# A two-block transformer on one core: the second block's attention takes its values as stationary operand in two parts, and norms the exponents on GpSimd ahead of the turn

## The chip, the cores and the metric

The kernel runs on one NeuronCore of one Trainium2 chip. The metric is the device time of one execution in microseconds. TensorE (PE) does matmuls and transposes, ScalarE (ACT) activations and copies, VectorE (DVE) elementwise work and reductions, GpSimd (POOL) small loads before this change, and SyncE (SP) issues the weight loads. Each engine runs its own list of instructions strictly in order and waits on semaphores for the others.

## What is computed

512 tokens of width 1024 go through a first block (2 layers) and a second block (2 layers). The change is in the second block's attention alone. Cut to that, for each of its layers:

```python
# fox: 8 heads of 64, causal, with a forget term
s = q @ k.T * scale + c_q[:, None] - c_k[None, :]
o_a = softmax(where(kpos <= qpos, s, -inf)) @ v
# nsa: 8 heads of 64, 2 kv heads; three branches, each with its own gate
o_c = (softmax(where(valid, q @ kc.T, NEG)) * valid) @ vc      # 31 compressed blocks
o_s = softmax(causal(q @ ks.T)) @ vs                           # "selected": all blocks at 512 tokens
o_w = softmax(causal(q @ kw.T)) @ vw                           # window of 512
o_n = g[..., 0:1] * o_c + g[..., 1:2] * o_s + g[..., 2:3] * o_w
mixed = sigmoid(gate_a) * (o_a @ w_o_fox) + sigmoid(gate_b) * (o_n @ w_o_nsa)
x = x + mixed @ w_out
```

## The kernel before

Dense layers run with each float32 operand split into an upper and a lower fp32r part, three matmuls for one (`three`, L568 to L570). Weights come in units of 512 KB; ScalarE makes the upper part `Wh` (L1273) and VectorE the lower part `Wl` (L1883), two units ahead of their use. A unit is 24 matmuls of 512 columns on TensorE.

The order of every engine is written out by hand with generators. The main thread of the program issues the dense layers, and after each 6 of its matmuls calls `tick()`, which lets every open side do one step. The attention is such a side: between two ticks stand 6 dense matmuls (3 short ones in `hidden`), which fill the time in which the attention's own steps wait for other engines. All engines run the same scheme, so that step i of a side stands at the same place of the main thread on each of them. `drain(side)` calls `tick()` with no dense matmuls between until that side is finished.

`attend` handles one item (t, g, h), a block of 128 queries and a head, with t+1 blocks of keys. In step i TensorE turns the exponents of item i-3 (`turn`, L713), makes the scores of item i (`head`, L781 to L784, mask L777) and mixes item i-5 (`mix`, L728). ScalarE makes the exponents of item i with their sum (L1394) and copies the turned exponents of even items out of PSUM (L1408); VectorE takes the maximum of item i (L2072) and copies those of odd items (L2085). In `mix` the turned exponents are stationary (128x128) and 64 columns of values move, all in float32. The sums are inverted once for all heads of a query block, and the output is scaled after the mixing (L2109, L2120), turned back (`turn_out`, L745; `on_side`, L792) and split for the next dense layer.

Per layer of the second block there are 32 fox items and 64 nsa items. The nsa side begins while the first gate layer runs and ends under the last gate layer; the three branches are added on VectorE in SBUF (L2123, L2712), and the compressed branch is a side of its own that runs at the same time (`compressed_side`, values at L1158):

```python
        for s in range(2):
            while (tag, 2 * c + s, 0) not in done:
                yield
            b = fresh(f"co{l} {2 * c + s}")
```

The main thread then waits for the outputs in front of the output projection:

```python
        drain(ont)
        for t in range(0, KD, 2):
            lin_t(f"ob{l} {t}", 4, M.ONh, M.ONl, at_each(f"on{l}") if t == 0 else None)
```

Of the kernel before, what the change touches and what calls it, by code (L numbers as in the profile page):

```python
# [8 lines left out]
F32 = mybir.dt.float32  # L9
# [158 lines left out]
class Memory:  # L168

    def __init__(self, nc, ctx):
# [18 lines left out]
        self.OS = fixed("OS", [2, 512])  # L190
        self.CST = fixed("CST", [C_END])
# [52 lines left out]
        self.QA = [area("QA", [4, S], w, F32R) for w in (6144, 0)]  # L244
        self.KAh = [area("KAh", [4, S], w, F32R) for w in (8192, 2048)]
        self.KAl = [area("KAl", [4, S], w, F32R) for w in (10240, 4096)]
        self.VF = area("VF", [NT, 512], 12288)
        self.OAh = area("OAh", [4, S], 14336, F32R)
        self.OAl = area("OAl", [4, S], 16384, F32R)
        self.FGT = area("FGT", [S], 14336)  # L250
# [4 lines left out]
        self.AK = area("AK", [2, 2, S], 8192)  # L255
        self.QNS = area("QNS", [NT, 512], 10240)
        self.KVS = area("KVS", [NT, 512], 12288)
# [3 lines left out]
        self.QN = area("QN", [8, S], 4096, F32R)  # L261
        self.KSh = area("KSh", [2, 2, S], 8192, F32R)
        self.KSl = area("KSl", [2, 2, S], 10240, F32R)
        self.ONS = area("ONS", [NT, 512], 18432)
# [19 lines left out]
        self.CT = area("CT", [512], 22688)  # L284
# [38 lines left out]
class Signals:  # L323

    def __init__(self, nc, ctx):
# [68 lines left out]
        self.ons = sem("nsa_branches_added")  # L395
# [105 lines left out]

def tiles(x):

    return x if isinstance(x, list) else [x[:, k, :] for k in range(x.shape[1])]
# [39 lines left out]
def tensor_program(pe, M, G, K, plan):  # L544
# [6 lines left out]
    used, pv = Count(G.w_used), Count(G.pv)  # L551
# [215 lines left out]

    def main_part(side, n):
# [10 lines left out]
    def causal(t, b, q, kh, kl, extra=None):  # L779
# [223 lines left out]
    for l in range(DEPTH):  # L1003
# [15 lines left out]
        def fox_scores(t, g, h, b):  # L1019
            return causal(t, b, M.QA[g][:, h, :], M.KAh[g][:, h, :], M.KAl[g][:, h, :], (M.SEL[0:96, 4 * g + h, :], M.CR[0:96, :]))  # L1020
# [10 lines left out]
        def fox_side(*args, **kw):  # L1031
            yield from idle(FOX_WAIT)
            yield from attend(*args, **kw)

        def heads_side(j):
# [7 lines left out]
            else:  # L1043
                pe.wait_ge(G.rk, 2 * l + j - 3)
                turn_rows(f"nk{l} {j - 4}", lambda s: M.KVS[:, s, 256 * (j - 4):256 * (j - 4) + P])
# [5 lines left out]
        def nsa_scores(t, g, h, b):  # L1051
            return causal(t, b, M.QN[:, h, :], M.KSh[:, g, h // 4, :], M.KSl[:, g, h // 4, :])

        def nsa_side():
# [15 lines left out]
            yield from attend(tag, softmax_items(8, (0, 1)), 8, nsa_scores,  # L1070
# [1837 lines left out]
```

## Time and profile before

| | us |
|---|---|
| runs, median of 3 | 2899.51 (2898.21 to 2901.87) |
| the profiled execution | 2900.79 |
| its span, first to last instruction | 2899.0 |
| TensorE busy in the span | 2797.7 |
| VectorE, ScalarE, GpSimd busy | 1435.8, 1161.7, 14.6 |
| granted TensorE clock, mean | 0.984 |

The span is what the trace shows; the 1.8 us around it are the launch. Busy times overlap: matmuls are pipelined, so the start of one to the start of the next is its price in a full stream, and the "mean ns" of one is longer than that. The second block's first layer lies at 1237 to 2080 us, its second one at 2080 to 2899 us, and the two read alike.

### The profile page before, as it was taken

To read this page: it belongs to the slowest core of one execution; us is meant where nothing else is said; L and a number is where in the kernel's file an instruction comes from. 1 tells how busy PE (TensorE), PEld (TensorE's weight loads), DVE (VectorE), ACT (ScalarE), POOL (GpSimd) and SP (SyncE) were. 2 spreads that over 40 slices of the span, in tenths; PEclk is the share of its full clock that TensorE was granted. 3 is DMA by queue.
4 is the path that set the end of the run, shared out by engine and by line. 5 is a ranking of instruction groups with operands and counts; after the bars stand their busy time and mean duration, and the time that the engine had idled before them with its cause. 6 is when DMAs were issued, how large, how long until landed. Compare 5 with 4: busy or idle time off the path is not lost.

```text
span 2899.0 us, 35141 instructions
## 1 busy us (share of the span) xinstructions
PE 2797.7 (97%) x14041; PEld 2316.3 (80%) x14041; DVE 1435.8 (50%) x2435; ACT 1161.7 (40%) x2009; POOL 14.6 (1%) x29
## 2 busy tenths in 40 slices
PE   7999999998999999989999999999999999999997
PEld 6777888887778888778788888888778788888886
DVE  6755433357553433465645553343556545553343
ACT  4554222235542222354656343242354655342231
POOL 1000000000000000000000000000000000000000
PEclk9899999999999999999999999999999999999999
DMA  4102333321023333321311223333312211333332
GB/s 131 43 23 87 95 95 101 95 82 51 23 80 95 101 95 95 91 62 53 97 51 45 87 88 95 101 95 95 84 52 81 73 37 59 98 94 100 95 97 71
DMA packets 186357, 231.43 MB, mean 80 GB/s; under 512 B 11874, under 2 KB 140356, under 8 KB 186196
## 3 DMA queue, kind: packets, MB, share of 16 engines
q1 hardware_dynamic: 184500, 225.95, 25.8%
q0 software_dynamic: 976, 1.32, 0.3%
q8 instruction: 112, 1.84, 0.3%
q10 hardware_dynamic: 720, 1.92, 0.2%
q14 instruction: 49, 0.40, 0.0%
HBM read 227.05 MB, written 2.11 MB: 79 GB/s over the span
## 4 chain that ended last, share of the span: by engine, by line
PE 84%; DVE 9%; ACT 4%; issue 3%; DMA 0%; DVEq 0%; ACTq 0%; SPq 0%
PE bank L568 24%; PE bank L570 24%; PE bank L569 23%; PE bank L728 4%; PE bank L713 2%; DVE Wl L1883 1%; ACT Wh L1273 1%; PE bank L781 1%; PE bank L782 1%; PE bank L665 1%; DVE KAl L1931 1%; PE bank L963 1%; DVE STT L2072 1%; ACT TMP L1394 0%; PE bank L777 0%
## 5 line engine op out<-in xcount | busy, mean ns | idle before, releaser
L1883 DVE TENSOR_TENSOR Wl<-RAW,Wh 128x1024 fp32r<-128x1024 f32 (+3 forms) x434 | 511.3, 1200 | 436.3 <-ACT Wh L1273 435.6
L1273 ACT ACTIVATE Wh<-RAW 128x1024 fp32r<-128x1024 f32 (+3 forms) x434 | 438.3, 1032 | 367.6 <-PE bank L570 367.4
L568 PE MATMUL bank<-Hh,Wh 128*128 128x512 f32 (+1 forms) x976 | 397.6, 407 | 6.6 <-DVE Wl L1883 5.0
L570 PE MATMUL bank<-Hh,Wl 128*128 128x512 f32 (+1 forms) x976 | 383.1, 392 | 0.0
L569 PE MATMUL bank<-Hl,Wh 128*128 128x512 f32 (+1 forms) x976 | 381.9, 391 | 0.0
L568 PE MATMUL bank<-Wh,A 128*128 128x512 f32 x864 | 337.2, 390 | 0.0
L570 PE MATMUL bank<-Wh,A 128*128 128x512 f32 x864 | 336.3, 389 | 0.0
L569 PE MATMUL bank<-Wl,A 128*128 128x512 f32 x864 | 336.2, 389 | 0.0
L568 PE MATMUL bank<-HA,Wh 128*128 128x512 f32 x704 | 276.1, 392 | 7.5 <-DVE HA L1932 7.5
L570 PE MATMUL bank<-HA,Wl 128*128 128x512 f32 x704 | 274.9, 390 | 0.0
L569 PE MATMUL bank<-HA,Wh 128*128 128x512 f32 x704 | 274.9, 390 | 0.0
L568 PEld LDWEIGHTS bank<-Hh,Wh 128*128 128x128 f32 (+1 forms) x976 | 183.4, 188 | 44.5 <-DVE Wl L1883 5.8
L1394 ACT ACTIVATE TMP<-bank,STT 128x512 f32<-128x512 f32 (+1 forms) x240 | 126.6, 529 | 229.0 <-DVE STT L2072 228.2
L570 PEld LDWEIGHTS bank<-Hh,Wl 128*128 128x128 f32 (+1 forms) x976 | 182.7, 187 | 41.6
L568 PE MATMUL bank<-Wh,Hh 128*128 128x512 f32 (+2 forms) x512 | 207.7, 406 | 4.1 <-DVE Wl L1883 2.7
L569 PEld LDWEIGHTS bank<-Hl,Wh 128*128 128x128 f32 (+1 forms) x976 | 183.5, 188 | 34.5
L570 PE MATMUL bank<-Wh,Hl 128*128 128x512 f32 (+2 forms) x512 | 195.0, 381 | 0.0
L569 PE MATMUL bank<-Wl,Hh 128*128 128x512 f32 (+2 forms) x512 | 194.0, 379 | 0.0
L570 PEld LDWEIGHTS bank<-Wh,A 128*128 128x128 f32 x864 | 162.2, 188 | 33.8
L569 PEld LDWEIGHTS bank<-Wl,A 128*128 128x128 f32 x864 | 162.2, 188 | 33.4
L568 PEld LDWEIGHTS bank<-Wh,A 128*128 128x128 f32 x864 | 162.2, 188 | 33.1
L568 PEld LDWEIGHTS bank<-HA,Wh 128*128 128x128 f32 x704 | 132.7, 188 | 36.6 <-DVE HA L1932 8.6
(357 smaller groups left out, 4133.4 us busy)
## 6 DMA issues: line engine op xcount, KB each, us to landing
RAW<-in_w_up_dram SPq DMA_DIRECT2D x108, 512.0 KB, 3.7
RAW<-in_w_down_dram SPq DMA_DIRECT2D x108, 512.0 KB, 3.7
RAW<-in_w_in_dram SPq DMA_DIRECT2D x90, 512.0 KB, 3.6
RAW<-in_w_gate_dram SPq DMA_DIRECT2D x44, 512.0 KB, 3.8
RAW<-in_w_out_dram SPq DMA_DIRECT2D x28, 512.0 KB, 3.7
RAW<-in_cmp_w_dram SPq DMA_DIRECT2D x16, 512.0 KB, 3.8
RAW<-in_w_o_fox_dram SPq DMA_DIRECT2D x8, 512.0 KB, 3.7
RAW<-in_w_o_nsa_dram SPq DMA_DIRECT2D x8, 512.0 KB, 3.4
```

The costliest lines, as they stand in the source:

```text
L568: pe.matmul(o, sh, mh, start=first, stop=False)
L569: pe.matmul(o, sh, ml, start=False, stop=False)
L570: return pe.matmul(o, sl, mh, start=False, stop=last)
L665: i = pe.transpose(b[:, s * P:(s + 1) * P], M.X[:, s, k * P:(k + 1) * P], ident)
L713: x = pe.transpose(b[:, k * P:(k + 1) * P], M.PB[:, i % 4, k * P:(k + 1) * P], ident)
L728: x = pe.matmul(b[:, h * 64:(h + 1) * 64], M.PT[:, i % 3, k * P:(k + 1) * P], values(g, h, kb[k]), start=k == 0, stop=k == len(kb) - 1)
L781: pe.matmul(b[:, 0:w], q[:, t * P:w], kh[:, 0:w], start=True, stop=False)
L782: pe.matmul(b[:, 0:w], q[:, t * P:w], kl[:, 0:w], start=False, stop=extra is None)
L963: pe.matmul(b[:, 0:w], M.MQ[0:96, h, t * P:w], M.MK[0:96, h, 0:w], start=True, stop=True)
L1273: sc.activation(M.Wh[:, v % NHL, 0:n], M.RAW[:, v % NRAW, 0:n], ACT.Copy).then_inc(G.w_hi, 1)
L1394: sc.activation(pb, b[:, 0:w], ACT.Exp, bias=nm, accum_out=sm).then_inc(*K.empties(name))
L1883: ve.tensor_tensor(M.Wl[:, v % NRAW, 0:n], M.RAW[:, v % NRAW, 0:n], M.Wh[:, v % NHL, 0:n].bitcast(F32), ALU.subtract).then_inc(G.w_lo, 1)
```

## The change

Work is arranged in bundles of two items: for fox two query blocks of a head, for nsa two heads of a query block. The exponents `P1` of an item are multiplied with one over their sum (and with the gate, for nsa) by GpSimd before they are turned. The turned ones are split in two fp32r parts, the upper by ScalarE and the lower by VectorE, for every item. In `mix` the values are stationary (128 columns: upper and lower part side by side) and the turned exponents of both items move (up to 256 columns); a second matmul with the upper values alone takes the lower part of the exponents. The output comes out already turned, with its two halves in PSUM rows 0 to 63 and 64 to 127, which ScalarE and VectorE add (`OAy`, `ONS`). The compressed branch is added in the same PSUM bank (`compressed_values`, four matmuls of 128 columns for one query block and kv head), at the last bundle of a bank. The nsa side on every engine waits before such a bundle until the compressed side is done.

The diff, cut to its core:

```diff
@@ PE @@
+    def mixing(B, scores, values, first_mix=None, group=None, extra=None, need=None):
+        def turn(i):
+            b = fresh(f"{tag} t{i}")
+            pe.wait_ge(*norm.due())
+            e = B.exps(M, i)
+            for k in range(len(B.blocks(i))):
+                x = pe.transpose(b[:, k * P:(k + 1) * P], e[:, k * P:(k + 1) * P], ident)
...
+        def mix(n):
...
+            if B.closes(n) and extra:
+                extra(*items[last], b)
...
+            for k in range(len(kb)):
+                ph, c = B.beside(M.PTh, n, k)
+                pl, _ = B.beside(M.PTl, n, k)
...
+                pe.matmul(b[:, c:c + w], v, ph, start=B.opens(n) and k == 0, stop=False, skip_group_check=True)
+                x = pe.matmul(b[0:64, c:c + w], v[:, 0:64], pl, start=False, stop=k == len(kb) - 1, skip_group_check=True)
...
+        for i in range(n + 7):
...
+            c = B.ended(i - 5)
+            if need and c is not None and B.closes(c):
+                while need not in done:
+                    yield
+            if 0 <= i - 3 < n:
+                turn(i - 3)
+            if i < n:
+                head(i)
+            if c is not None:
+                mix(c)
+            yield
-        pe.matmul(b[:, 0:w], q[:, t * P:w], kl[:, 0:w], start=False, stop=extra is None)
+        pe.matmul(b[:, 0:w], q[r:r + 64, t * P:w], kl[r:r + 64, 0:w], start=False, stop=extra is None)
-                for s in range(2):
-                    while (tag, 2 * c + s, 0) not in done:
-                        yield
-                    b = fresh(f"co{l} {2 * c + s}")
...
+            done.add(("compressed", l))
@@ on_side @@
-            for j in range(4):
-                turn_rows(f"on{l} {j}", lambda s: M.ONS[:, s, j * P:(j + 1) * P])
@@ ACT @@
+            upper(B.turned(M.PTh, i), M.bank[K.of(name)][:, 0:len(B.blocks(i)) * P].rearrange("p (k c) -> p k c", c=P), name)
+        def fox_take(t, g, h):
+            sc.activation(M.OAy[64 * (h % 2):64 * (h % 2) + 64, 2 * g + h // 2, :], M.bank[K.of(o)][0:64, :], ACT.Copy).then_inc(G.whole, 1)
@@ DVE @@
+        def invert(n):
+            i = B.ends[n] - 1
+            (t0, _, h0), (t1, _, h1) = B.bundles[n]
+            sums, fac = (M.STT[:, x, t0:t1 + 1, h0:h1 + 1] for x in (1, 4))
+            ve.wait_ge(*K.drained(f"{tag} s{i}"))
+            ve.reciprocal(fac, sums).then_inc(*rec.up())
+        def turn(i):
+            lower(B.turned(M.PTl, i), M.bank[K.of(name)][:, 0:len(B.blocks(i)) * P].rearrange("p (k c) -> p k c", c=P),
+                  B.turned(M.PTh, i)).then_inc(*K.empties(name))
...
+            if 0 <= i - 3 < n:
+                turn(i - 3)
+            c = B.ended(i - 1)
+            if c is not None:
+                invert(c)
+            if i < n:
+                head(i)
@@ fox_k, lower part of the keys @@
-                    for r in (0, 64):
-                        i = lower(M.KAl[c][r:r + 64, 2 * j + x, :], M.TQ[64 * x:64 * x + 64, j, :], M.KAh[c][r:r + 64, 2 * j + x, :])
+                    r = slice(64 * x, 64 * x + 64)
+                    i = lower(M.KAl[c][r, j, :], M.TQ[r, j, :], M.KAh[c][r, 2 * j + x, :])
@@ POOL @@
+    def normalise(B, gate):
+        for i, (t, g, h) in enumerate(B.items):
+            if B.place[i][1] == 0:
+                gp.wait_ge(*rec.due())
+            e = B.exps(M, i)
+            fac = M.STT[:, 4, t, h:h + 1]
+            if gate(t, g, h) is None:
+                gp.tensor_scalar(e, e, fac, None, ALU.mult).then_inc(G.norm, 1)
+            else:
+                gp.tensor_scalar(e, e, fac, gate(t, g, h), ALU.mult, ALU.mult).then_inc(G.norm, 1)
```

In the changed kernel's lists the dense matmuls are L643 to L645, the turn is L858, scores L921 and L922, mask L916, mixing L879 (upper) and L880 (lower), compressed values L1299. `P_9` is the exponents, `PT_58` and `PT_59` the two parts of the turned ones.

First, TensorE at the end of the nsa side. Before, near the end of the side of the first layer:

```order
L713 MATMUL bank<-CST_57,TMP_55 128x128 x3
L728 MATMUL bank<-KVS_117,TMP_55 128x64 x3
L568 MATMUL bank<-Hh_50,Wh_54 128x512
L569 MATMUL bank<-Hl_51,Wh_54 128x512
L570 MATMUL bank<-Hh_50,Wl_53 128x512
L568 MATMUL bank<-Hh_50,Wh_54 128x512
L569 MATMUL bank<-Hl_51,Wh_54 128x512
L570 MATMUL bank<-Hh_50,Wl_53 128x512
L713 MATMUL bank<-CST_57,TMP_55 128x128 x2
```

Now, at the same end:

```order
L858 MATMUL bank<-CST_61,P_9_57 128x128 x3
L921 MATMUL bank<-KSh_130,QN_129 128x384
L922 MATMUL bank<-KSl_131,QN_129 128x384
L916 MATMUL bank<-CMB_65,IDB_64 128x128
L879 MATMUL bank<-PT_58,VN_122 128x256
L880 MATMUL bank<-PT_59,VN_122 64x256
L879 MATMUL bank<-PT_58,VN_122 128x256
L880 MATMUL bank<-PT_59,VN_122 64x256
L858 MATMUL bank<-CST_61,P_9_57 128x128 x2
L921 MATMUL bank<-KSh_130,QN_129 128x384
L922 MATMUL bank<-KSl_131,QN_129 128x384
L916 MATMUL bank<-CMB_65,IDB_64 128x128
```

Before, every step had its 6 dense matmuls. Now the side stops after 18 heads (it waits for the compressed side), 30 steps come later with dense matmuls, and the last 17 heads and 20 turns of each layer stand in `drain(ont)` with none between them.

Second, ScalarE and VectorE at the start of a unit of weights in the nsa side (second step after a pair's last exponents). ScalarE before:

```order
L1394 ACTIVATE TMP_55,STT_65<-bank,STT_65 128x128
L1273 ACTIVATE Wh_54<-RAW_52 128x1024
L1394 ACTIVATE TMP_55,STT_65<-bank,STT_65 128x384
L1408 ACTIVATE TMP_55<-bank 128x512
L1394 ACTIVATE TMP_55,STT_65<-bank,STT_65 128x256
```

ScalarE now:

```order
L1582 ACTIVATE P_9_57,STT_69<-bank,STT_69 128x128
L1448 ACTIVATE PT_58<-bank 128x4x128
L1582 ACTIVATE P_9_57,STT_69<-bank,STT_69 128x128
L1402 ACTIVATE Wh_54<-RAW_52 128x1024
L1448 ACTIVATE PT_58<-bank 128x4x128
L1582 ACTIVATE P_9_57,STT_69<-bank,STT_69 128x512
```

VectorE now, at the same place:

```order
L2137 TENSOR_TENSOR PT_59<-bank,PT_58 128x4x128
L2368 TENSOR_REDUCE STT_69<-bank 128x1
L2089 TENSOR_TENSOR Wl_53<-RAW_52,Wh_54 128x1024
L2137 TENSOR_TENSOR PT_59<-bank,PT_58 128x4x128
L2376 RECIPROCAL STT_69<-STT_69 128x2
L2368 TENSOR_REDUCE STT_69<-bank 128x1
```

Both splits of a unit now stand between the last exponents of a pair and the reciprocal of its sums, and a copy of turned exponents is on each engine in every step.

## Rows read from the trace of the kernel before

**Rows 1.** The page: span, and busy time of the engines.

```profile
span 2899.0 us, 35141 instructions
PE 2797.7 (97%) x14041; PEld 2316.3 (80%) x14041; DVE 1435.8 (50%) x2435; ACT 1161.7 (40%) x2009; POOL 14.6 (1%) x29
```

**Rows 2.** Busy time by stretch: stretch and length, busy of each engine, PEclk.

```profile
core 0: us, PE busy (x) PEld busy (x) DVE busy (x) ACT busy (x) POOL busy (x), PEclk, DMA share, GB/s
1237.00:1290.00 53.00, 44.60 (x223) 34.93 (x222) 40.02 (x62) 30.93 (x52) 0.00 (x0) 1.00 0.21 61
1290.00:1390.00 100.00, 99.39 (x588) 82.35 (x587) 53.83 (x103) 43.54 (x93) 0.00 (x0) 1.00 0.21 63
...
1430.00:1500.00 70.00, 66.87 (x436) 56.55 (x436) 32.53 (x70) 45.41 (x95) 0.00 (x0) 0.98 0.19 53
1500.00:1570.00 70.00, 69.80 (x432) 58.94 (x433) 38.95 (x78) 36.08 (x72) 0.00 (x0) 0.97 0.14 39
```

**Rows 3.** The chain of waits in 1237 to 1286 us, shares by line.

```profile
by line: DVE KAl L1931 22.3%; DVE Wl L1883 11.8%; issue 7.2%; ACT KAh L1688 5.1%; ACT Wh L1273 4.1%; DVE TQ L2020 4.1%; DVE STT L2072 3.3%; ACT TMP L1394 2.9%; DVE TMP L2521 2.8%; DVE QA L1931 2.8%; DVE TQ L2022 2.7%; ACT QA L1680 2.6%; ACT
```

**Rows 4.** Groups of instructions on PE by shape, both layers (a float32 matmul leaves two records).

```profile
L728 PE MATMUL bank<-KVS,TMP 128*128 128x64 f32 x640 | 92.5, 275 | 0.1
...
L728 PE MATMUL bank<-VF,TMP 128*128 128x64 f32 x320 | 45.5, 273 | 0.0
...
L1158 PE MATMUL bank<-VCB,CT 128*128 128x256 f32 x32 | 8.8, 396 | 0.4 <-DVE CT L2697 0.4
...
L792 PE MATMUL bank<-CST,ONS 128*128 128x128 f32 x32 | 4.9, 275 | 1.9 <-DVE ONS L2123 1.9
```

**Rows 5.** The chain of waits over the whole run: start, us, what.

```profile
1280.86 0.89 PE bank L728 x8
...
1525.76 0.92 PE bank L1158 x4
```

**Rows 6.** Timeline of PE, short dense matmuls: start, us, what.

```profile
1463.43 0.28 PE L569 MATMUL bank<-Wl,XHL 128*64 128x256 f32 x1
1463.55 0.28 PE L570 MATMUL bank<-Wh,XHL 128*64 128x256 f32 x1
1463.67 0.38 PE L713 MATMUL bank<-CST,TMP 128*128 128x128 f32 x2
```

**Rows 7.** Timeline of one nsa step at the start of a unit.

```profile
1518.28 0.60 PE L713 MATMUL bank<-CST,TMP 128*128 128x128 f32 x4
...
1518.92 0.60 ACT L1408 ACTIVATE TMP<-bank 128x512 f32<-128x512 f32 x1 [0.60 <-PE bank L713]
...
1519.17 0.29 DVE L2072 TENSOR_REDUCE STT<-bank 128x1 f32<-128x128 f32 x1 [0.57 <-PE bank L777]
1519.49 0.37 ACT L1394 ACTIVATE TMP<-bank,STT 128x128 f32<-128x128 f32 x1
...
1519.85 1.05 ACT L1273 ACTIVATE Wh<-RAW 128x1024 fp32r<-128x1024 f32 x1
...
1520.93 1.23 DVE L1883 TENSOR_TENSOR Wl<-RAW,Wh 128x1024 fp32r<-128x1024 f32 x1 [1.47 <-ACT Wh L1273]
...
1521.69 0.27 PE L713 MATMUL bank<-CST,TMP 128*128 128x128 f32 x1
```

**Rows 8.** Groups on ACT, 1237 to 1570 us.

```profile
L1394 ACT ACTIVATE TMP<-bank,STT 128x512 f32<-128x512 f32 x24 | 16.5, 689 | 44.0 <-DVE STT L2072 44.0
...
L1394 ACT ACTIVATE TMP<-bank,STT 128x384 f32<-128x384 f32 x20 | 11.6, 582 | 33.2 <-DVE STT L2072 33.2
L1805 ACT ACT_TABLE_LOAD x9 | 11.5, 1283 | 0.2
```

**Rows 9.** Groups on DVE, 1237 to 1570 us.

```profile
L1931 DVE TENSOR_TENSOR KAl<-TQ,KAh 64x512 fp32r<-64x512 f32 x16 | 11.0, 687 | 3.0 <-ACT KAh L1688 2.8
L2072 DVE TENSOR_REDUCE STT<-bank 128x1 f32<-128x384 f32 x20 | 11.1, 553 | 1.2 <-PE bank L777 0.9
...
L2098 DVE RECIPROCAL STT<-STT 128x4 f32<-128x4 f32 x8 | 1.4, 171 | 0.1
```

**Rows 10.** Timeline of PE about a fall of the clock.

```profile
1496.73 0.28 PE L1132 MATMUL bank<-KCh,QN 128*128 128x32 f32 x1 [0.23 <-ACT TMP L1394]
...
1502.08 0.63 PE L570 MATMUL bank<-OAh,Wl 128*128 128x512 f32 x1
```

**Rows 11.** Groups on POOL over the whole run.

```profile
L2897 POOL MEMSET const-bfloat16-1.0<- 128x1 bf16 x1 | 0.1, 96 | 0.0
```

More of the change, by code:

```diff
@@ L1 @@
 import collections
+import itertools
 from contextlib import ExitStack
@@ L499, in softmax_items, with __init__, blocks, opens @@
     return [(t, g, h) for g in groups for pair in PAIRS for h in range(heads) for t in pair]
+class Bundles:
+    def __init__(self, tag, bundles, out, col):
+        self.tag, self.bundles, self.col = tag, bundles, col
+        self.items = [item for b in bundles for item in b]
+        self.place = [(n, x) for n, b in enumerate(bundles) for x in range(len(b))]
+        self.ends = list(itertools.accumulate(len(b) for b in bundles))
+        self.outs = [f"{tag} o{out(*b[0])}" for b in bundles]
+    def blocks(self, i):
+        return key_blocks(self.tag[:3], self.items[i][0])
+    def opens(self, n):
+        return self.outs[n] not in self.outs[:n]
+    def closes(self, n):
+        return self.outs[n] not in self.outs[n + 1:]
+    def ended(self, i):
+        return self.ends.index(i + 1) if i + 1 in self.ends else None
+    def span(self, i):
+        n, x = self.place[i]
+        first = i - x
+        at = n % 2 * (1536 - 512 * len(self.bundles[n]) // 2 if len(self.bundles[n]) == 2 else 768)
+        lo = at + sum(len(self.blocks(j)) * P for j in range(first, i))
+        return lo, lo + len(self.blocks(i)) * P
+    def exps(self, M, i):
+        lo, hi = self.span(i)
+        return M.P1[:, lo:hi]
+    def freed_by(self, i):
+        n, lo, hi = self.place[i][0], *self.span(i)
+        return max((j for j in range(i) if self.place[j][0] == n - 2 and self.span(j)[0] < hi and lo < self.span(j)[1]), default=None)
+    def turned(self, part, i):
+        n, x = self.place[i]
+        m = len(self.bundles[n])
+        at = self.span(i - x)[0]
+        nb = len(self.blocks(i - x + m - 1))
+        return part[:, at:at + nb * m * P].rearrange("p (k x c) -> p k x c", x=m, c=P)[:, 0:len(self.blocks(i)), x, :]
+    def beside(self, part, n, k):
+        b, i = self.bundles[n], self.ends[n] - len(self.bundles[n])
+        x = [len(self.blocks(i + y)) > k for y in range(len(b))].index(True)
+        at = self.span(i)[0] + k * len(b) * P
+        return part[:, at + x * P:at + len(b) * P], self.col(*b[x])
@@ L502, in tiles, with fox_bundles, nsa_bundles @@
+def fox_bundles(l):
+    pairs = [[(t, g, h) for t in pair] for g in range(2) for h in range(4) for pair in ((2, 3), (0, 1))]
+    return Bundles(f"fox{l}", pairs, lambda t, g, h: f"{g}{h}", lambda t, g, h: t * P)
+def nsa_bundles(l):
+    pairs = [[(t, g, h), (t, g, h + 1)] for pair in PAIRS for kv in range(2) for g in range(2) for h in (4 * kv, 4 * kv + 2) for t in pair]
+    return Bundles(f"nsa{l}", pairs, lambda t, g, h: f"{t}{h // 4}", lambda t, g, h: h % 4 * P)
 def tiles(x):
@@ L1731, in nsa_side @@
             yield from idle(5)
-            yield from attend(tag, softmax_items(8, (0, 1)), 8, None)
+            yield from mixing(nsa_bundles(l), take=nsa_take, need=("compressed", l))
         def hidden(kv):
@@ L2620, in nsa_side @@
             yield from idle(5)
-            yield from attend(tag, softmax_items(8, (0, 1)), 8, None)
+            yield from mixing(nsa_bundles(l), add_up=nsa_sum, need=("compressed", l))
         def hidden(kv):
```

334 lines of the change are left out of this document (235 added, 99 removed).

## Prediction, made before the changed kernel ran

> **What bounds the kernel now.** I read the page first: TensorE is busy in 2797.7 of 2899.0 us [rows 1], so time taken from its stream is time gained, unless something else moves in. Next the busy time by stretch. In the fox stage (1290 to 1390 us) TensorE is busy 99.39 of 100 us, and where nsa runs under dense layers 69.80 of 70 us, while ScalarE and VectorE are about half busy [rows 2]. The reader should see that half-busy engines cause no wait today because each has two to three steps of slack: exponents of item i are turned at step i+3, copies are used at step i+5. At the front of fox (1237 to 1290 us) it is otherwise: 8.4 us idle on TensorE [rows 2], and the chain of waits runs through VectorE, with `KAl` the largest piece [rows 3]. So three questions decide: what leaves TensorE's stream, whether the new chain of waits still fits the slack, and whether dense matmuls still stand between the steps.
>
> **TensorE's own work, per layer.** Old mixing leaves 640 and 320 records over both layers [rows 4], 480 a layer, at 0.89/8 = 0.111 us [rows 5]: 53 us. New mixing, counted from the diff: 160 matmuls for nsa and 64 for fox with 256 columns, 32 for fox with 128. The trace has no such matmul of a value tile, but the short dense ones with 256 moving fp32r columns start 0.12 us apart [rows 6]. A bound from below is half of it for the 64-column stationaries (128 matmuls, 8 us less), from above 0.15. I take 0.12: 31 us, 22 saved. The turns of the outputs (16 for nsa, 16 for fox) go: 32 records of `ONS` in both layers [rows 4], about 0.09 each, so 3 us. The compressed values cost 16 records of 0.92/4 = 0.23, 4 us at most [rows 4, 5]; now 32 float32 matmuls of 128 columns, 64 records at the 0.11 of L728, 7 us: 4 lost. Sum: 21 us less a layer, **42 us less**. The shorter contraction of `kl` I cost at nothing: the same columns move.
>
> **The front of fox.** 8 of 16 `KAl` instructions of 0.69 us go [rows 9], on the engine that is the chain there; the split of the fox values adds about 1.4 us to it earlier. I take 3.5 us a layer, **7 us less**; bounds 0 and 5.5.
>
> **The new chain.** The step in front of the turn is now: last exponents of a pair (ScalarE), copy of the turned item before it (ScalarE), its lower part and then the reciprocal (VectorE, in this order in its list), norm (GpSimd), turn (TensorE). From the start of an odd step I add rows [rows 7, 9]: 0.64 until the copy of four turned blocks starts, copy 0.60, lower part 0.69 (a VectorE instruction of 512 columns), maximum 0.29, exponents 0.37, and, where a unit begins there, `Wh` 1.05 and `Wl` 1.23, then the next lower part 0.69, reciprocal 0.17, norm. GpSimd's multiplication is in no row. Below it lies its memset, 0.1 us [rows 11]; above it `Wl`, which is twice as long in elements and two-input, 1.23 us. I take what VectorE needs for the same shapes, 0.3 us at 128 columns and 0.55 to 0.7 above [rows 7, 9], being the nearest. With some 0.3 us of hand-overs this is 6.3 us, 3.8 without the splits. The two TensorE steps that must cover it hold 12 dense matmuls of 0.23 and 1.9 us of attention, 4.7 us. So an ordinary pair is hidden, and each unit of weights that begins between the last exponents and the reciprocal costs 1.5 us. Queued behind the waiting turn are the scores, and behind these everything of the next step.
>
> The Trainium skill (GPSIMD Engine Reference, section 3.1) gives 769 ns for one input of 512 elements; by it the norm of the longest items would be 0.1 us longer than mine and the sum about 3 us higher, an estimate. No row here shows it.
>
> Fox: the pieces are wider (exponents of four blocks 0.69 [rows 8], scores with four matmuls) and a 64-row copy of the output stands ahead of `Wh`: 6.9 us against 5.2 of cover. 7 units fall so: **12 us a layer**. In the first 18 steps of nsa two stretches of four steps have only 3 short dense matmuls (0.36 us), so a pair has 2.7 us of cover against 3.8 to 4; with four unit starts I take **9 us a layer** net of what waits there now (3.1 us idle, [rows 2]). The 30 later filled steps have the units at the harmless place in the pair, but both sigmoids of each gate layer, with table loads of 1.28 us on either side [rows 8], stand ahead of a copy or the next exponents: some 3 us in 8 steps, **10 us a layer**. Together 31 a layer, **62 more**.
>
> **The end of nsa without cover.** The side stops after 18 heads until the compressed side is done, about 30 ticks. These dense matmuls are then missing at the end: 17 heads and 20 turns a layer stand in `drain(ont)` alone. A pair is now its chain: turn and scores 0.7, reading 0.2, maximum 0.5, exponents 0.53 (between 384 and 256 columns, [rows 8, 9]), copy 0.45, lower part 0.5, reciprocal 0.17, norm 0.45, hand-overs 0.3: 3.8 to 4 us, ten pairs, 39 us. TensorE's work in it is 23 us (50 turned blocks at 0.107, 17 scores at 0.45, 54 mixings at 0.12, compressed values 3.6). So 16 us idle, plus 2.4 at the end, where the last copy, the sum and two splits stand in front of the output projection, which before were hidden by the last gate layer (none of it idle today, [rows 2]): 18.4 a layer, **37 more**.
>
> **The clock.** Today a stretch of small matmuls after short idle times is followed by one at the lower level: at 1502.08 us a 512-column matmul takes 0.63 us [rows 10] where 0.40 is usual, and the clock means 0.98 and 0.97 there [rows 2]. The uncovered end is 40% idle, so I expect it to fall there, partly under the chain's own waits, and one fall of today to be gone: net 2 a layer, **4 more**.
>
> **The sum.** 2899.0 - 42 - 7 + 62 + 37 + 4 = 2953 us of span; with the 1.8 us around it 2955. The profiled execution (2900.79) is 1.3 us above the median of the runs (2899.51). Hence **2954 us**, 1.9% slower.
>
> **Rivals.**
> *Only the savings* (faster, 6%): the waits stay hidden, the end too. 2899.5 - 49 = 2851 us. For it: engines half busy. Against: latency, not busy time, is what the new chain lacks; ScalarE was already waited for when it only had exponents.
> *Only the uncovered end costs* (10%): in the filled steps the split of a unit finds room, because ScalarE runs ahead of TensorE. Then -49 + 37 + 4: 2892 us. It decides on the 1.5 us: if `Wh` could begin before the odd step's exponents, there is no stall. The list has it behind them.
> *Longer norms and a low clock* (20%): GpSimd at the upper bound, 0.5 more in each of some 35 binding pairs a layer (+32), and the whole end at 1.2 GHz, turn and scores doubled in ten pairs and some us after it (+18): 3004 us. A mechanism for the first part is VectorE holding what GpSimd reads through: 38 `Wl` of 1.23 us lie among 333 us, and a norm behind one waits up to that long. The Trainium skill (SBUF — State Buffer, section "SBUF: two separate sides") states such an exclusive lock between a VectorE instruction with two SBUF inputs and a GpSimd instruction; no run here has shown it, for GpSimd computes nothing today.
> *The gain and the loss cancel* (4%).
> The forecast has the remaining 60%; its own range is 2920 to 2985 (chain stalls between half and one and a half times mine).
>
> **Numbers.** The range takes in the forecast, the case with the uncovered end alone, and most of the one with longer norms: 2890 to 3010. What repeats of this kernel can tell from no change is about 0.2%, 6 us. Slower: 0.60 + 0.20 + a little = 0.81; within 0.2% 0.05; faster 0.14, from the first two rivals.
>
> **What would show it.** Right: L879 and L880 start 0.12 us apart; idle of TensorE ahead of L858, ended by GpSimd, of 1 to 2 us at unit starts in fox; an end of nsa of about 40 us a layer with TensorE some 60% busy, ahead of the output projection; GpSimd busy 80 to 150 us; no idle at the compressed side. Wrong: if L858 never waits in fox, the chain is shorter than I added; if mixing takes 0.2 us a matmul, the saving is gone and the time lies above 2985; if the end of nsa is under 30 us a layer, the pair's chain overlaps more than I think.

## The result, and the profile after

The changed kernel takes **3053.99 us** (median, 3052.99 to 3055.3), the kernel before 2898.95 us beside it: ratio 1.0533, 95% interval 1.0515 to 1.0551. It is 5.3% slower where 1.9% was forecast, and lies outside the range of 2890 to 3010 us. The direction was right, the size was not.

The page of the profile after, the lines that answer to [rows 1]:

```profile
span 3051.2 us, 34802 instructions
PE 2855.3 (94%) x13625; PEld 2309.7 (76%) x13625; DVE 1476.4 (48%) x2551; ACT 1225.5 (40%) x2166; POOL 163.2 (5%) x221
```

There are 416 fewer TensorE records than before, and yet TensorE is busy 58 us longer. So two things went wrong at once: its own work did not shrink, and it idles besides. To see both, I cut the first layer into the stretch from the first fox score to the last and the stretch from the first nsa score to the output projection. After (the third row is the end of nsa that has no dense matmuls to cover it, without its first wait: the last dense matmul ends at 1639.6 us), then before, as busy time by stretch:

```profile
core 0: us, PE busy (x) PEld busy (x) DVE busy (x) ACT busy (x) POOL busy (x), PEclk, DMA share, GB/s
1262.60:1379.70 117.10, 94.10 (x463) 68.70 (x463) 57.54 (x111) 56.35 (x127) 32.75 (x30) 0.93 0.13 37
1439.50:1696.40 256.90, 224.09 (x1102) 168.97 (x1102) 115.74 (x252) 135.42 (x282) 38.45 (x64) 0.89 0.15 44
1643.50:1696.40 52.90, 44.05 (x187) 30.83 (x186) 21.58 (x56) 23.13 (x68) 10.92 (x19) 0.65 0.00 0
```

```profile
1263.70:1355.00 91.30, 85.72 (x522) 69.28 (x523) 49.04 (x93) 47.87 (x109) 0.00 (x0) 1.00 0.16 47
1415.90:1620.30 204.40, 199.03 (x1229) 167.21 (x1230) 103.32 (x207) 115.53 (x228) 0.00 (x0) 0.98 0.18 51
```

Fox is 26 us longer and nsa 52.5. Idle (length less busy) grew from 5.6 to 23.0 us in fox and from 5.4 to 32.8 us in nsa: 45 of the 78. The granted clock fell from 1.00 and 0.98 to 0.93 and 0.89, and to 0.65, mostly the 1.2 GHz level, in the uncovered end. The rest is busy time, longer in part by that clock. By start-to-start times of the records, idle taken off, in these stretches (mixing in fox before includes 0.8 us of turned outputs):

| us, first layer | before | after |
|---|---|---|
| scores with `kh` and `kl`, fox / nsa | 11.8 / 25.3 | 21.6 / 50.5 |
| mixing, fox / nsa | 14.7 / 34.9 | 9.7 / 29.2 |
| compressed values | 3.0 | 9.0 |
| turns of exponents, fox / nsa | 6.2 / 13.9 | 7.4 / 17.5 |
| dense, fox / nsa | 46.2 / 104.6 | 49.7 / 104.3 |

The scores stand out: 35 us more a layer, in a part that the prediction costed at nothing. TensorE's longest waits after:

```profile
engine line waited for: us in total, times, longest us
PE bank L858 <- POOL P L3128: 54.9, 47, 4.1
PE bank L858 <- POOL P L3126: 30.0, 16, 9.5
PE bank L921 <- DVE OAy L2833: 7.4, 6, 1.3
PE bank L1285 <- DVE CB L2970: 7.4, 4, 2.6
```

L858 is the turn and waits for GpSimd's norm, 85 us in both layers; the prediction had the place and 62 us of such stalls. The fourth row is the turn of the compressed branch's exponents, which waited for nothing before. What a norm takes, by shape (x and mean ns of one):

```profile
L3126 POOL TENSOR_SCALAR P<-P,STT 128x512 f32<-128x512 f32 x16 | 27.8, 1740 | 0.0
L3128 POOL TENSOR_SCALAR P<-P,STT,GS 128x512 f32<-128x512 f32 x32 | 24.4, 771 | 289.4 <-DVE STT L2376 289.4
...
L3128 POOL TENSOR_SCALAR P<-P,STT,GS 128x128 f32<-128x128 f32 x32 | 14.1, 450 | 96.9 <-DVE STT L2376 96.9
L3126 POOL TENSOR_SCALAR P<-P,STT 128x128 f32<-128x128 f32 x16 | 9.6, 603 | 60.6 <-DVE STT L2376 60.6
```

The nsa form, with two scalars, takes 771 ns at 512 columns. The Trainium skill gives 769 ns, measured, for 512 elements of one input at best (GPSIMD Engine Reference, section 3.1), and the trace agrees. The fox form, with one scalar, takes 1740 in the mean, which neither that page nor my range had.

One stall of fox, start to end, in the timeline after (start, us, engine):

```profile
1317.30 0.69 ACT L1582 ACTIVATE P<-bank,STT 128x512 f32<-128x512 f32 x1 [1.43 <-DVE STT L2368]
...
1317.81 0.38 PE L858 MATMUL bank<-CST,P 128*128 128x128 f32 x2
...
1318.10 0.59 ACT L1883 ACTIVATE OAy<-bank 64x512 f32<-64x512 f32 x1
...
1318.54 0.36 PE L879 MATMUL bank<-PT,VF 128*128 128x256 f32 x1
1318.72 1.06 ACT L1402 ACTIVATE Wh<-RAW 128x1024 fp32r<-128x1024 f32 x1
...
1318.74 0.28 PE L880 MATMUL bank<-PT,VF 128*64 128x256 f32 x1
1318.86 0.28 PE L879 MATMUL bank<-PT,VF 128*128 128x256 f32 x1
...
1319.68 0.37 ACT L1448 ACTIVATE PT<-bank 128x256 fp32r<-128x256 f32 x1
...
1319.81 1.23 DVE L2089 TENSOR_TENSOR Wl<-RAW,Wh 128x1024 fp32r<-128x1024 f32 x1 [0.39 <-ACT Wh L1402]
...
1321.07 0.42 DVE L2137 TENSOR_TENSOR PT<-bank,PT 128x256 fp32r<-128x256 f32 x1
1321.41 0.16 DVE L2376 RECIPROCAL STT<-STT 128x2 f32<-128x2 f32 x1
...
1321.66 3.26 POOL L3126 TENSOR_SCALAR P<-P,STT 128x384 f32<-128x384 f32 x2 [5.90 <-DVE STT L2376]
...
1323.05 0.52 PE L858 MATMUL bank<-CST,P 128*128 128x128 f32 x3 [2.00 <-POOL P L3126]
```

The reader should see that the exponents are ready at 1318.0 and the norm begins at 1321.66: the output's copy, `Wh`, the turned copy, `Wl` and the lower part stand ahead of a reciprocal of 0.16 us. That is the chain that the prediction named. (The mixing in between starts 0.20 us apart once and then 0.12.)

### The profile page after: what moved, and what is told of

Same layout as the page of the kernel before. It is cut to its first block and busy times, and to the rows that moved or that the text cites. A ratio compares the mean times of both kernels' runs of the same rounds, so it can differ in the third digit from the quotient of the medians.

```text
span 3051.2 us, 34802 instructions
## 1 busy us (share of the span) xinstructions
PE 2855.3 (94%) x13625; PEld 2309.7 (76%) x13625; DVE 1476.4 (48%) x2551; ACT 1225.5 (40%) x2166; POOL 163.2 (5%) x221
## 5 line engine op out<-in xcount | busy, mean ns | idle before, releaser
L643 PE MATMUL bank<-Hh,Wh 128*128 128x512 f32 (+1 forms) x976 | 394.3, 404 | 5.9 <-DVE Wl L2089 4.3
L645 PE MATMUL bank<-Hh,Wl 128*128 128x512 f32 (+1 forms) x976 | 385.3, 395 | 0.0
L643 PE MATMUL bank<-Wh,A 128*128 128x512 f32 x864 | 337.2, 390 | 0.0
L645 PE MATMUL bank<-Wh,A 128*128 128x512 f32 x864 | 336.3, 389 | 0.0
L643 PE MATMUL bank<-HA,Wh 128*128 128x512 f32 x704 | 276.7, 393 | 7.2 <-DVE HA L2138 7.2
L645 PE MATMUL bank<-HA,Wl 128*128 128x512 f32 x704 | 275.5, 391 | 0.0
L643 PEld LDWEIGHTS bank<-Hh,Wh 128*128 128x128 f32 (+1 forms) x976 | 184.9, 189 | 45.4 <-DVE Wl L2089 5.1
L645 PEld LDWEIGHTS bank<-Hh,Wl 128*128 128x128 f32 (+1 forms) x976 | 184.3, 189 | 41.6
L643 PE MATMUL bank<-Wh,Hh 128*128 128x512 f32 (+2 forms) x512 | 206.7, 404 | 4.1 <-DVE Wl L2089 2.7
L2137 DVE TENSOR_TENSOR PT<-bank,PT 128x384 fp32r<-128x384 f32 (+1 forms) x192 | 94.3, 491 | 229.6 <-ACT PT L1448 228.7
L645 PE MATMUL bank<-Wh,Hl 128*128 128x512 f32 (+2 forms) x512 | 195.0, 381 | 0.0
L645 PEld LDWEIGHTS bank<-Wh,A 128*128 128x128 f32 x864 | 162.2, 188 | 33.8
L643 PEld LDWEIGHTS bank<-Wh,A 128*128 128x128 f32 x864 | 162.2, 188 | 33.2
L858 PE MATMUL bank<-CST,P 128*128 128x128 f32 x480 | 99.2, 311 | 89.8 <-POOL P L3128 54.9
```

What stands on the lines that cost most here:

```text
L643: pe.matmul(o, sh, mh, start=first, stop=False)
L645: return pe.matmul(o, sl, mh, start=False, stop=last)
L858: x = pe.transpose(b[:, k * P:(k + 1) * P], e[:, k * P:(k + 1) * P], ident)
L2137: return ve.tensor_tensor(lo, src, h.bitcast(F32), ALU.subtract)
```

## The experiments

All ratios are to the kernel before, run beside them, with their 95% intervals. e7, e8, e9, e15 and e17 leave out parts of the result and only measure; the others compute all of it. "Beyond the bound" means that the intervals of two kernels don't overlap.

### The contraction of `kl`

```
e1: the changed kernel
-        pe.matmul(b[:, 0:w], q[r:r + 64, t * P:w], kl[r:r + 64, 0:w], ...)
+        pe.matmul(b[:, 0:w], q[:, t * P:w], kl[:, 0:w], ...)
e2, e2b: the kernel before
-        pe.matmul(b[:, 0:w], q[:, t * P:w], kl[:, 0:w], ...)
+        pe.matmul(b[:, 0:w], q[0:64, t * P:w], kl[0:64, 0:w], ...)     # e2
+        pe.matmul(b[:, 0:w], q[0:96, t * P:w], kl[0:96, 0:w], ...)     # e2b
```

> The changed kernel with one edit: the matmul with the lower parts of the keys contracts over all 128 rows again (it then adds the query's lower part times the lower part of the other head's keys, a term of the size of rounding). Theory A (the 64-row matmul costs, because every item pays some 0.28 us more from score to score, 96 items a layer): the 512-column kl matmul goes back from 0.43 to about 0.24 us start to start and the kernel loses about 50 us, to 3000 to 3010 us. Rival B (the 64-row matmul only fills time in which TensorE would have waited for GpSimd): waits for GpSimd grow by as much, and the time stays at 3040 to 3055 us.

> The kernel before with one edit: its kl matmul contracts over rows 0 to 63 alone, as in the change; what it leaves out is the product of the two lower parts. Theory A: in this kernel, where TensorE is the bound, it costs 0.28 us an item, 192 items, so about 54 us: 2950 us. Rival (the extra time belongs to the change of row halves between heads or to another row of the new order): no more than 5 us, 2900 to 2905 us.

> The kernel before with its kl matmul over rows 0 to 95, as the forget-gate matmul of fox already does with its 96 rows. If any contraction below 128 rows costs, this gives the same as the 64-row one, about 2950 us. If only one of at most 64 rows does, since the 96-row forget-gate matmul next to it never showed more than its columns, 2900 us.

Measured: e1 3031.63 us (1.0464, 1.0443 to 1.0486), 22 us less; e2 2938.51 (1.0138, 1.0122 to 1.0154), 39 us more in a kernel that has nothing else of the change; e2b 2900.1 (1.0004, 0.9994 to 1.0013), no change. One item in the timeline of e2, then the same item in e2b:

```profile
1290.13 0.42 PE L781 MATMUL bank<-KAh,QA 128*128 128x384 f32 x1
1290.48 0.44 PE L782 MATMUL bank<-KAl,QA 64*128 64x384 f32 x1
1290.86 0.34 PE L784 MATMUL bank<-CR,SEL 96*128 96x384 bf16 x1
```

```profile
1289.28 0.42 PE L781 MATMUL bank<-KAh,QA 128*128 128x384 f32 x1
1289.54 0.34 PE L782 MATMUL bank<-KAl,QA 96*128 96x384 f32 x1
1289.72 0.34 PE L784 MATMUL bank<-CR,SEL 96*128 96x384 bf16 x1
```

From L781 to L782 0.35 us instead of 0.26, from L782 to L784 0.38 instead of 0.18: 0.29 us for this item. By the medians of e2 against before it is 0.28 to 0.29 us at 256 to 512 columns and 0.23 at 128, so it hardly grows with the columns. The Trainium skill has a rule for it (TensorEngine Tiling (Array Packing), section "Tiling Modes", key properties: changing the tiling mode drains the TensorE; 64 rows are a mode, 96 are not one). For rows the runs agree; the same section lists stationaries of 64 columns as a mode too, and there they show no such price (L879 and L880 alternate at 0.12 us above). Over e2 the scores grew by 52 us, 0.27 an item, and 9 us less idle time took part of it back: 39. In e1 the busy time of both stretches fell by 30 us a layer, but their length by only 8.5, since idle took its place: the turns now waited 121 us for GpSimd instead of 85. So theory A had the mechanism, and B's waits took more than half of it back: the time lies between the ranges of the two. In the kernel before, 39 us came where A said 54.

### The norm and what stands around it

From here all start from e1 with a second scalar in the norm of fox (e4), but for e3, which has the second scalar alone; where GpSimd's norm is left out, there is no second scalar to add.

```
e3, e4 (GpSimd):
-                gp.tensor_scalar(e, e, fac, None, ALU.mult)
+                gp.tensor_scalar(e, e, fac, 1.0, ALU.mult, ALU.mult)
e5 (VectorE): invert(c) goes ahead of turn(i - 3); e6: behind head(i) and add_up of the pair's last step
e8: the turn waits for the exponents
-            pe.wait_ge(*norm.due())
+            pe.wait_ge(*K.drained(f"{tag} s{i}"))
     and GpSimd's normalise(...) is left out
e10: e5, and on TensorE head(i) ahead of turn(i - 3)
e11: e5, and behind ve.reciprocal(...), in place of GpSimd, for both items:
+                ve.tensor_scalar(e, e, M.STT[:, 4, t, h:h + 1], gate(...), ALU.mult, ALU.mult).then_inc(G.norm, 1)
     (in fox with the one scalar alone)
```

> The changed kernel with one edit: the norm of the fox items on GpSimd gets a second scalar, 1.0, and so the form that the nsa items have. Theory B1 (the form with one scalar is the slow one: 1740 ns at 512 columns against 771): L3126 falls to 771, 663, 557 and 450 ns, the waits for it (30 us over both layers) go nearly all, and the time falls by 20 to 30 us, to 3025 to 3035. Rival B2 (GpSimd is slowed in fox by what VectorE does beside it): the form changes nothing, 3054 us.

> The changed kernel with the edits of the first and the fourth run together (kl over 128 rows, the two-scalar norm for fox); the later runs start from it. If the two add up: 3054 - 22 - 5 = 3027 us. With kl shorter the norm binds more often, so the second edit may be worth more than alone: 3015 to 3027. If the norm's length is hidden in fox whatever TensorE does, 3031 as with the first alone.

The second scalar made the norm of 512 columns 690 ns instead of 1740 (e4). Time: e3 3048.71 us (1.0518, 1.0502 to 1.0535), 5 us less and not beyond the bound; e4 3021.19 (1.0416, 1.04 to 1.0431), 10 us under e1 and beyond it, as expected (3015 to 3027). So theory B1 was right that the form is the slow thing, and wrong on its worth: 38 us less of GpSimd gave 5 and 10 us, not 20 to 30. In fox the norm is only the last piece of its chain.

> 128 rows and two scalars, and on VectorE the reciprocal of a finished pair stands ahead of the lower part of the turned item (it stood behind it). Theory N (TensorE waits on one chain: exponents, copy, lower part, reciprocal, norm, turn): the copy, the lower part and the hand-over between them leave the chain wherever no unit of weights stands ahead; waits L858 <- POOL fall from some 115 us to 50 to 70, the time to 2960 to 2985 us. Rival (the waits are set by the copies and exponents of the other items, the norm only comes last): waits move to other names, the time stays within 10 us of the kernel with the two edits.

> As the run before, but the reciprocal stands at the end of the pair's last step, ahead of the units of weights that begin behind that step. Theory N: the 1.2 us of Wl leave the chain too, so it lies another 10 to 20 us below the run before, 2945 to 2970 us. Rival W: VectorE now waits for the exponents (0.4 to 0.7 us) before each unit's Wl and all that follows it, so the dense stages get their weights and copies later; then this is slower than the run before, 2980 us or more.

e5 3001.25 us (1.0345, 1.0329 to 1.0362), 20 under e4; e6 3004.9 (1.036, 1.0345 to 1.0375), not to be told from e5. In e5 the waits for GpSimd fell from 118 to 97 us, not to 50 to 70, and the time lies between theory and rival. In e6 they fell further, to 85 us, but TensorE's busy time rose by 8, and the time stayed. The timeline of e6 shows something that worked against the move:

```profile
1299.46 0.15 DVE L2376 RECIPROCAL STT<-STT 128x2 f32<-128x2 f32 x1
...
1299.71 2.22 POOL L3126 TENSOR_SCALAR P<-P,STT 128x384 f32<-128x384 f32 x2 [6.34 <-DVE STT L2376]
1299.80 1.57 DVE L2089 TENSOR_TENSOR Wl<-RAW,Wh 128x1024 fp32r<-128x1024 f32 x1 [0.18 <-ACT Wh L1402]
```

and the norms of 512 columns in e6, grouped:

```profile
L3126 POOL TENSOR_SCALAR P<-P,STT 128x512 f32<-128x512 f32 x16 | 22.6, 1414 | 0.0
```

`Wl` takes 1.57 us instead of 1.23, the two norms together 2.22 where 0.58 and 0.69 are usual, and the mean of the long ones rose from 0.69 (e4) to 1.41 us. So each was held up by the other. The norms of fox grew by 12 us in all and 17 `Wl` took 1.56 to 1.66 us each. Rival W also said 2980 us or more, for another reason (VectorE waits for the exponents); no run tells how much of e6 is the one and how much the other.

> The changed kernel with kl over 128 rows and without the norm on GpSimd: the turn waits for the item's exponents alone (what this leaves out is the division by the sums and the gates). Theory N: the 118 us for which L858 waits for GpSimd come back but for what the exponents themselves cost; the wait shows as L858 <- ACT, some 20 us, and the time is 3021 - 100 = 2920 us, 2910 to 2945. Rival B (banks: the output's copy and sum hold a bank that the next scores, turns or mixings want): of 118 us only half comes back, 2950 us or more, with the waits <- DVE OAy grown.

e8 2987.12 us (1.0304, 1.0286 to 1.0321): 34 under e4, where I expected 100. Rival B was nearer (less than a third of the 118 us came back, where it said half), and more than banks came up:

```profile
PE bank L858 <- ACT P L1582: 23.5, 30, 2.5
PE bank L921 <- DVE PT L2137: 13.7, 15, 2.4
PE bank L858 <- DVE OAy L2833: 12.2, 2, 6.1
PE bank L879 <- DVE OAy L2833: 9.8, 4, 4.3
```

> 128 rows, two scalars, the reciprocal ahead of the lower part, and on TensorE the scores of a step ahead of its turn (they stood behind it). Theory N: the norm gets the 0.5 to 0.9 us of the scores as further cover at every step, and the maximum of the next item no longer waits behind a late turn: 40 or so waits get 0.7 us shorter, 2970 to 2980 us. Rival: exponents of item i write where item i-3 stood, so they wait for the turn that is now later, and the chain only turns round: 3000 us as before.

> 128 rows, the reciprocal ahead of the lower part, and the norm made by VectorE right behind the reciprocal instead of by GpSimd. Theory: what the norm costs is mostly its length (0.45 to 0.77 us an item, 1.1 to 1.4 a pair) and the hand-over; VectorE, half busy, takes 0.1 to 0.3 us an item, so waits of L858 fall by some 30 us: 2965 to 2980 us. Rival: VectorE's list gets longer, maxima and lower parts come later by as much: 2995 to 3010 us.

e10 3016.02 us (1.04, 1.0385 to 1.0416), 15 slower than e5: exponents wait for the later turn (L921 and L858 wait 21.9 us for ScalarE's exponents, 2.1 in e5). e11 3029.26 (1.0446, 1.0431 to 1.0462), 28 slower than e5: VectorE's norm took longer than I thought,

```profile
L2381 DVE TENSOR_SCALAR P<-P,STT,GS 128x512 f32<-128x512 f32 x32 | 16.0, 544 | 0.6
```

and L858 waited 99.1 us for it. Both moves cost, as their rivals had it, and both more than the rivals said (3000, and 2995 to 3010 us).

### The compressed branch in PSUM

```
e7 (from e4), e9 (from e8):
-            yield from mixing(nsa_bundles(l), ..., extra=compressed_values, need=("compressed", l))
+            yield from mixing(nsa_bundles(l), ...)
```

> 128 rows and two scalars, and the nsa side neither adds the compressed branch nor waits for it (what this leaves out is the compressed branch of the output). Theory E (the uncovered end costs on its own): nsa has no pause, the stretch between the last dense matmul and the output projection falls from some 50 us a layer to under 15, the 32 matmuls (7 us a layer) go, and the low clock behind it; the same heads now run under dense matmuls. Saved per layer: about 20 us of low clock and idle at the end, 7 of matmuls: 2965 to 2975 us. Rival: the chain is as long under dense matmuls, waits spread over the heads, and only the 7 us a layer are saved: 3010 us.

> As the run before, and the compressed branch neither added nor waited for (left out: the division, the gates, the compressed branch). The prediction's savings of 49 us should show here alone, with about 8 more for the compressed values: 2850 us for the first forecast's savings. If ScalarE still binds, 2860 to 2880 us; over 2900 would say that the savings were sized wrongly.

e7 2987.82 us (1.03, 1.0283 to 1.0317), 33 under e4; e9 2957.36 (1.0199, 1.0184 to 1.0214), 30 under e8. The two agree with each other, and lie between theory and rival of e7. What came back is mostly busy time. From e9 to e8 TensorE is busy 31 us more and idle as long as before (190 us of the span in both), although the uncovered end, which e9 doesn't have, is idle for 16 us a layer in e8: with all heads under dense matmuls, the same idle time stands elsewhere. From e7 to e4 it is 23 us busy and 12 idle. e9 was the surprise: without norm, gates, compressed branch and 64-row matmul the new arrangement is still 57 us slower than before, where the savings alone should have shown. Its idle time is that of the full change, 20.5 and 32.1 us:

```profile
1262.10:1367.30 105.20, 84.67 (x464) 66.21 (x464) 56.05 (x110) 55.63 (x127) 0.00 (x0) 0.92 0.14 41
1426.50:1646.30 219.80, 187.71 (x1038) 150.68 (x1037) 114.17 (x253) 130.61 (x279) 0.00 (x0) 0.95 0.17 48
```

### What holds the rest: banks, or two engines for each item

```
e12 (from e5; ScalarE, VectorE): take and add_up at ended(i - 5), not ended(i - 6); e15: the same from e9
e13 (from e5; TensorE): K.close(o) of a finished output two steps later; e14: e12 and e13; e16: e6 and e13
e17 (from e9):
-            upper(B.turned(M.PTh, i), ..., name)            # ScalarE, each item
+            if i % 2 == 0: sc.activation(B.turned(M.PTh, i), ..., ACT.Copy).then_inc(*K.empties(name))
-            lower(B.turned(M.PTl, i), ...)                  # VectorE, each item
+            if i % 2: ve.tensor_copy(B.turned(M.PTh, i), ...).then_inc(*K.empties(name))
-                pl, _ = B.beside(M.PTl, n, k)               # TensorE, second matmul
+                pl, _ = B.beside(M.PTh, n, k)
```

> 128 rows, two scalars, the reciprocal ahead of the lower part (3001 us so far), and ScalarE's copy and VectorE's sum of a finished output one step earlier, so its bank is drained some 2 to 4 us sooner. Theory K (banks): waits <- DVE OAy and ONS, 22 us, fall under 8, the clock behind them stays up, 2980 to 2990 us. Rival A (ScalarE's list): the copy now stands ahead of a turned copy and of the next exponents and makes the chain to the norm longer by its 0.6 us: 3000 to 3010 us.

> The same start (3001 us), and the bank of a finished output goes back to the row of free banks two steps later than its last mixing, so that it comes round again after it was read; the others come round sooner. Theory K: waits <- DVE OAy and ONS go, 2980 to 2990 us. Rival: with one bank less in the row the others (scores, turned items, dense outputs) are wanted before they are drained, 3005 us or more.

> Both edits of the two runs before on the same start. By theory K the second adds little to the first (the waits go once): 2980 to 2990 us. If both cost by their rivals, 3010 us or more.

> The kernel without norm and compressed branch (2957 us; left out: the division, the gates, the compressed branch), with copy and sum of the outputs one step earlier. By theory K 26 us of waits <- OAy and ONS go and some clock with them: 2925 to 2935 us. If ScalarE's list is what holds, 2950 to 2960. If neither, the rest is the turned items' own chain (copy, lower part) and the clock.

> 128 rows, two scalars, the reciprocal at the pair's end and the output banks given back two steps later. If the two gains of 16 and 5 us simply add: 3021 - 16 - 5 = 3000 us. If the later bank removes what held the pair-end version (its waits <- DVE OAy, 16 us): 2985 to 2995 us. In no case does the order of the lists bring it near 2900.

e12 3008.4 us (1.0371, 1.0356 to 1.0387), e13 2996.01 (1.0329, 1.0312 to 1.0346), e14 3009.5 (1.038, 1.0365 to 1.0396), e15 2951.78 (1.0178, 1.0163 to 1.0193), e16 2995.79 (1.0334, 1.0317 to 1.0351). In e12 and e13 the waits for the outputs' banks went from the top of the list, but those for GpSimd grew from 97 to 113 and 108 us: the copy that comes earlier costs 7 us, which lies in rival A's range, and a bank that comes back later gains 5, both within the bound; the two together (e14) are slower than e5 just beyond it. In e15 the earlier copy brought the waits for the outputs from 47 to 8 us and the time down by 6, within the bound, where theory K said 22 or more. So the outputs' banks alone are not what holds. e13 and e16 are the fastest complete versions, 3.3% slower than before; none that does all the work beats the kernel before.

> The kernel without norm and compressed branch (2957 us; left out: the division, the gates, the compressed branch), with the turned exponents copied whole by ScalarE for even items and by VectorE for odd ones, as before the change; the second matmul of each block moves the same tile again, so TensorE's work is unchanged (left out besides: the lower parts of the exponents). Theory S (the split is the rest): idle falls from 53 to under 25 us a layer, the clock rises with it, 2880 to 2910 us. Rival O (the order of the items, two long ones in a row and then two short ones, holds it, or the banks): 2940 us or more.

e17 2916.63 us (1.0057, 1.004 to 1.0073), 41 under e9:

```profile
1261.60:1358.00 96.40, 82.25 (x462) 65.14 (x463) 50.77 (x96) 49.37 (x113) 0.00 (x0) 0.96 0.15 44
1416.80:1627.80 211.00, 187.88 (x1038) 152.81 (x1037) 101.23 (x221) 118.81 (x247) 0.00 (x0) 0.94 0.17 51
```

TensorE's busy time is that of e9 (-2.2 us over the two), its idle time fell from 52.6 to 37.3. The time lies 7 us above theory S's range and under rival O's; the idle time did not fall under 25. So the split costs 41 us, and it is not all of the rest. It puts two engines behind each other on every item where one of two was enough, but it also gives them more work (VectorE and ScalarE are busy 18 us less each in these stretches of e17); no run parts the two.

## Why the prediction was wrong

The runs make a ladder from before to after, one part at a time (what each costs depends on the order, since TensorE waits for whichever chain is longest):

| | us | step | TensorE busy, idle |
|---|---|---|---|
| before | 2899 | | 2798, 101 |
| values stationary, one copy per item, no norm, no compressed branch (e17) | 2917 | +18 | 2763, 151 |
| exponents split in two parts, one engine behind the other (e9) | 2957 | +41 | 2764, 190 |
| compressed branch in PSUM, with the pause (e8) | 2987 | +30 | 2795, 190 |
| norm with two scalars on GpSimd (e4) | 3021 | +34 | 2793, 229 |
| the one-scalar form in fox (e1) | 3032 | +10 | 2793, 237 |
| `kl` over 64 rows (after) | 3054 | +22 | 2855, 196 |

The last column is of the profiled executions, idle being the span less the busy time. The rung of e17 is flattered: it leaves out the division, the gates and the compressed values, which the kernel before makes. The change cost 155 us where 54 were forecast. Of the 101 missing, by this ladder, 81 lie in the first rung, 23 in the split and the norm, 22 in `kl`, and the compressed branch was 25 cheaper than forecast.

- **"The shorter contraction of `kl` I cost at nothing: the same columns move."** This step failed outright. It costs 0.27 us an item in the mean, 96 items a layer: 26 of the 35 us by which the scores grew. The rest is put down to the lower clock, since the medians are those of e2. Alone it costs 39 us, as the last rung 22, because there it fills time in which TensorE would have waited: 63 us more busy, 41 less idle.
- **TensorE's own work, 42 us less.** The mechanism was right, the size not. Mixing fell from 49.6 to 38.9 us in the first layer, not by 22: the first 256-column matmul of a group takes 0.20 us to the next, not 0.12, where it stands behind the bf16 mask L916 (72 times in the changed kernel's trace; behind a dense fp32r matmul, twice, 0.11), and the last groups ran at the lower clock. In e17, without the uncovered end, it takes 33. The compressed values took 9.0 us for 3.0, a loss of 6, not 4. The bigger mistake is that the savings were set against the stalls as if apart. For what e17 has of the change the prediction's terms give 49 us less, and 14 more for the compressed values that it leaves out: 56 of TensorE's work and 7 at the front. Measured, TensorE is busy 35 us less and idle 50 us more, so e17 is 18 us above before. In the two stretches 37 us of idle time a layer stand where 11 stood, though nothing waits for a norm or a lower part. The prediction put the idle time of the bare rearrangement at nothing, and gave no reason.
- **The new chain, 62 more.** The place and the order were right: `Wh`, copy, `Wl`, lower part, reciprocal, norm ahead of L858, and e5 gained 20 us by one move in it. The terms were mis-sized. The norm had 0.55 to 0.7 us at 512 columns and took 1.74 in fox and 0.77 in nsa. The split, which I counted only as two pieces of the chain to the norm, costs 41 us with no norm at all. With 34 and 10 for the norm the chain is 85. In the first layer of the changed kernel the waits for GpSimd under dense matmuls are 35 us, near the 31 that the prediction had, but by luck: the 64-row matmuls fill 36 us of such waits (121 in both layers of e1, 85 here). Two sums of the prediction don't come out either, and change little: without the splits its pieces add to 4.0 us, not 3.8, and its 10 us for the later steps of nsa isn't worked out from the 3 us that it names.
- **The end of nsa without cover, 37 more, and the clock, 4.** Together with all of the compressed values (7 in each layer, which e7 and e9 leave out) that is 55; taking all of it out gave 30 to 33. The end is 57 us in the first layer from the last dense matmul on, not 39 and 2.4, with 11 us idle, not 18: TensorE was busy 44 us of the row above for what I had at 23, at a granted clock of 0.65 and with 64-row scores. With 128-row scores (e4) the end is 55 us with 22 idle. The last part of "longer norms and a low clock", the whole end at 1.2 GHz, came true for most of it. The step that failed is to count the end's idle time as added: from e9 to e8 no idle time is added in all. The sign "no idle at the compressed side" did not come either: its turn L1285 waits 7.4 us.
- **The front of fox, 7 less.** The first score comes at 1262.6 us instead of 1263.7: 1 us a layer. The first turn then waits 9.5 us for its norm, behind `KAl` and a unit, so the front is a loss: from 1237 to 1290 us TensorE is idle for 12.5 us, before for 8.4.
- **The rival with VectorE's lock.** In the changed kernel no `Wl` ran beside a norm, and the reciprocal stands behind `Wl` in VectorE's list; e6, which moved it, showed the lock. The lower part of a fox output, with two SBUF inputs as well, does run beside norms: in 6 of the 16 of 512 columns the norm took 2.04 instead of 1.56 us, 3 us in all.

What is still open, then, is the largest piece: what holds e17 above before (the order, in which two long items follow each other and then two short ones; the output's copy and sum by two engines; the two-item buffers of the exponents), and what the clock costs by itself. No run took these apart. Of e17's 37 us of idle time in the two stretches of the first layer, its trace ends 16 with the outputs' sums (`OAy`, `ONS`), some 11 with exponents, 7 with turned copies on VectorE and 4 with the compressed branch's exponents; e15 warns that a wait that is taken out comes back under another name.

## What to carry to other kernels

Compare how many engines touch each item one behind the other before and after, not only their busy shares: half-busy engines hid one copy per item, but not a copy and a subtraction of each. Before a stall is costed by one chain, ask what waits next when it is gone: the norm carried 118 us of waits, and taking it out gave 34. And a matmul's shape is part of its price: shortening a contraction from 128 to 64 rows saved nothing and cost 0.23 to 0.29 us each time.

## What the chip showed that I had not expected

- A 64-row matmul among 128-row ones starts some 0.09 us later behind the matmul ahead of it, and the next one starts some 0.20 us later behind it (384 columns, e2 against e2b); 96 rows cost nothing, and neither do the 64-column stationaries of L880, which alternate with 128-column ones at 0.12 us for 256 columns.
- GpSimd's multiplication by one scalar per row took 603 ns for 128 columns and 1560 for 512 (1740 in the mean of all 16, with those that were held up beside VectorE); with a constant 1.0 as second scalar 690 at 512, with two scalars from SBUF 768 to 771.
- A GpSimd norm and a VectorE instruction with two SBUF inputs that overlap hold each other up: `Wl` took 1.57 instead of 1.23 us, and the long norms 1.41 instead of 0.69 us in the mean, in e6. The Trainium skill states this as an exclusive lock (SBUF — State Buffer, section "SBUF: two separate sides"); the trace agrees.
